# The end of each expert search moved from VectorE to GpSimd, with a store, the features, one search and six gathered steps placed elsewhere

## The reference

```python
q = (xb @ w_query).reshape(t, PEER_HEADS, 2, HALF_KEY)
s = jnp.einsum('thik,hink->thin', q, sub_keys)
v_half, i_half = lax.top_k(s, TOPK)                                # 16 best of 128 keys, in both halves
cand = v_half[:, :, 0, :, None] + v_half[:, :, 1, None, :]         # 16 x 16 pairs
cand_idx = i_half[:, :, 0, :, None] * N_KEYS + i_half[:, :, 1, None, :]
top_v, top_pos = lax.top_k(cand, TOPK)                             # 16 best pairs
idx = jnp.take_along_axis(cand_idx, top_pos, axis=-1)              # the expert's number
g = jax.nn.softmax(top_v, axis=-1)
act = jax.nn.gelu(jnp.einsum('thkd,td->thk', expert_u[idx], xb))
out = jnp.einsum('thk,thkd->td', g * act, expert_v[idx])
```

## Time and profile before

| | us |
|---|---|
| Three runs | 2607.22, 2611.05, 2610.92 (median 2610.92) |
| The profiled execution | 2620.58 |
| Its span | 2618.8 |
| First 64 u blocks on TensorE | 1458 to 1701 |
| Gates built | 1702 to 1837 |
| Rest of the u blocks and half of the v blocks | 1839 to 2283 |
| Last v blocks | 2283 to 2510 |
| End of the last gathered steps and results | 2619 |

### The profile page before, as it was taken

The page is one execution under the profiler, slowest core; times in us unless marked ns, Lnnn a source line. Parts: engine busy times, 40 slices in busy tenths (PEclk is TensorE's granted clock), DMA queues, the critical chain, the costliest instruction groups (busy, mean ns, idle before and its releaser), DMA issues.

```text
span 2618.8 us, 26507 instructions
## 1 busy us (share of the span) xinstructions
PE 2305.7 (88%) x8779; PEld 1454.0 (56%) x8779; DVE 1801.4 (69%) x3184; ACT 638.1 (24%) x1564; POOL 1169.0 (45%) x978
## 2 busy tenths in 40 slices
PE   6988888998899998899989988977999999999930
PEld 1545454454467443477568877856666666644410
DVE  2657676645501888777778997578766676757698
ACT  2334435331211113311321112199111100100010
POOL 0022222221000347666532334556548878676675
PEclk8999999999999998899999999999999999999975
DMA  8211101117575669999775679989999999999998
GB/s 303 73 33 57 40 24 40 49 60 272 195 269 182 229 254 383 361 339 415 287 265 185 225 257 334 348 305 362 352 394 411 412 386 418 347 419 378 419 395 296
DMA packets 235577, 705.28 MB, mean 269 GB/s; under 512 B 22910, under 2 KB 47614, under 8 KB 234052
## 3 DMA queue, kind: packets, MB, share of 16 engines
q0 software_dynamic: 117792, 428.92, 42.6%
q1 hardware_dynamic: 116948, 272.27, 27.9%
q10 hardware_dynamic: 720, 2.62, 0.2%
HBM read 690.23 MB, written 13.50 MB: 269 GB/s over the span
## 4 chain that ended last, share of the span: by engine, by line
PE 37%; DVE 19%; POOL 14%; DMA 11%; issue 11%; ACT 7%; SPq 1%; DVEq 0%; ACTq 0%; POOLq 0%; another core or an unknown queue 0%
PE bank L959 14%; POOL arena L1786 6%; POOL arena L1778 5%; DMA arena<-in_peer_v,arena 5%; PE bank L1181 4%; PE bank L808 4%; DMA arena<-in_peer_u,arena 3%; PE bank L853 2%; ACT arena L1674 2%; DVE arena L1964 2%; PE bank L1111 2%; DVE arena L2181 2%; POOL arena L1832 2%; DVE arena L2203 2%; DVE arena L2127 1%
## 5 line engine op out<-in xcount | busy, mean ns | idle before, releaser
L1778 POOL DMA_INDIRECT arena<-in_peer_u,arena x384 | 486.3, 1266 | 624.7 <-DVE arena L2181 346.0
L2203 DVE SCALAR_TENSOR_TENSOR arena<-arena 128x1024 f32<-128x1024 f32 x381 | 498.4, 1308 | 123.2 <-DMA arena<-in_peer_v,arena 113.6
L2181 DVE CUSTOM_DVE_ANT_0 arena<-arena 128x1024 f32<-128x1024 f32 x384 | 475.9, 1247 | 149.5 <-DMA arena<-in_peer_u,arena 147.5
L1786 POOL DMA_INDIRECT arena<-in_peer_v,arena x384 | 462.0, 1203 | 242.0 <-DVE arena L2203 132.4
L959 PE MATMUL bank<-arena 128*128 128x512 f32 (+1 forms) x1472 | 510.5, 509 | 21.8 <-issue 8.1
L1181 PE MATMUL bank<-arena 128*128 128x256 f32 x2048 | 457.2, 381 | 18.5 <-ACT arena L1633 17.8
L1219 PE MATMUL bank<-arena 128*128 128x512 f32 x1024 | 455.8, 598 | 7.2 <-DMA arena<-in_peer_v 4.0
L1181 PEld LDWEIGHTS bank<-arena 128*128 128x128 f32 x2048 | 391.7, 191 | 101.0 <-issue 49.4
L959 PEld LDWEIGHTS bank<-arena 128*128 128x128 f32 x1472 | 284.1, 194 | 244.1 <-issue 206.3
L1219 PEld LDWEIGHTS bank<-arena 128*128 128x128 f32 x1024 | 196.4, 192 | 228.1 <-issue 217.1
L1633 ACT ACTIVATE arena<-bank 128x256 f32<-128x256 f32 x128 | 49.0, 384 | 597.1 <-PE bank L1181 535.1
(11 more groups left out here) (259 smaller groups left out, 2469.6 us busy)
## 6 DMA issues: line engine op xcount, KB each, us to landing
arena<-in_peer_ut SPq DMA_DIRECT2D x128, 512.0 KB
arena<-in_peer_v SPq DMA_DIRECT2D x128, 512.0 KB
arena<-in_w_in SPq DMA_DIRECT2D x22, 2048.0 KB
arena<-in_w_ada_t POOLq DMA_DIRECT2D x32, 512.0 KB, 3.8
arena<-in_w_ssd_out SPq DMA_DIRECT2D x8, 2048.0 KB
arena<-in_w_query SPq DMA_DIRECT2D x8, 2048.0 KB
arena<-in_w_ada SPq DMA_DIRECT2D x4, 2048.0 KB, 16.3
arena<-in_w_fourier SPq DMA_DIRECT2D x4, 2048.0 KB
```

Source lines behind the costliest of these rows:

```text
L1778: nc.gpsimd.indirect_dma_start(rowbuf[slot], None, a["peer_u"], bass.IndirectOffsetOnAxis(ap=entries(IDX, k), axis=0)).then_inc(row_in[slo ...
L1786: nc.gpsimd.indirect_dma_start(rowbuf[slot], None, a["peer_v"], bass.IndirectOffsetOnAxis(ap=entries(IDX, k), axis=0)).then_inc(row_in[slo ...
L2181: V.tensor_tensor_reduce(out=rowbuf[slot], in0=rowbuf[slot], in1=h2c if item < PH else h2a[:, item // PH - 1, :], scale=1.0, scalar=0.0, o ...
L2203: STT(pv, rowbuf[slot], w, pv, ALU.mult, ALU.add).then_inc(s("vc_used"), 1)
```

## The change

1. **The search's end.** VectorE stops after the compare. It now casts the places to bf16 (L2237) and compares them with a table `places` of bf16 that is laid out in full, 16 wide (L2239). It raises `marked`. For the gathered tiles the numbers of the first half are multiplied by 128 while they are cast (`radix`). GpSimd does the rest in `picks_for`: multiply (L1819), adds of 8, 4 and 2 groups (L1821), and a last add into the whole numbers (L1823), or two adds and a cast into the rows' indices (L1826, L1828, L1829). Each waits for the one before it. VectorE waits for the end of one search before it overwrites the numbers in the next.
2. **Where GpSimd does it.** Ahead of each row's issue, all searches that VectorE passes before it frees that row's place are completed. The function `searches_before` works this out from a list of all searches.
3. **The store** of tile 0 goes from ScalarE's block 24 to GpSimd's apart step 28, with a semaphore of its own.
4. **The features** and the waits at ScalarE's block 31 go to block 35. `SOFTMAX_AT` goes from 8 to 10.
5. **44 steps** lie in the build instead of 38, and the search of heads 6 and 7 of tile 1 moves from step 94 to step 51, ahead of the build. What stands behind the build moves six steps with it.

The table `places` and several constants now share one buffer, `scan_consts`; the table is built just before the first search.

The core of the diff:

```diff
-SOFTMAX_AT = 8
+SOFTMAX_AT = 10
-IN_BUILD = 38
+IN_BUILD = 44
-APART_TOP_AT = {42 if n == 4 else START_BETWEEN if n == 6 else 16 * n - 14: (n, n + 1) for n in range(4, 2 * PH, 2)}
+APART_TOP_AT = {42 if n == 4 else 51 if n == 6 else 16 * n - 14: (n, n + 1) for n in range(4, 2 * PH, 2)}
...
-                if n == 24:
-                    store(0, 1)
-                if n == 31:
+                if n == 35:
                     act.wait_ge(s("topw_done"), 2 * PH)
...
+            def picks_for(kind, k):
+                while picks_done[0] < searches_before(kind, k):
+                    m, (items, _, _) = next(picked)
+                    n, (t, h) = len(items), divmod(items[0], PH)
...
+                    pool.wait_ge(s("marked"), m + 1)
+                    pch(TT(e4, e4, number.unsqueeze(3).broadcast_to([P, 2 * n, TOPK, TOPK]), ALU.mult))
+                    for m_left in (8, 4, 2):
+                        pch(TT(e4[:, :, 0:m_left], e4[:, :, 0:m_left], e4[:, :, m_left:2 * m_left], ALU.add))
+                    if t in WHOLE:
+                        TT(ij_all[:, :, TOPK * h:TOPK * h + TOPK], e4[:, :, 0, :], e4[:, :, 1, :],
+                           ALU.add).then_inc(s("topw_done"), n)
+                    else:
+                        pch(TT(picks[:, 0:2 * n * TOPK].rearrange("p (g k) -> p g k", g=2 * n), e4[:, :, 0, :], e4[:, :, 1, :],
+                               ALU.add))
+                        pch(TT(picks[:, 0:n * TOPK], picks[:, 0:n * TOPK], picks[:, n * TOPK:2 * n * TOPK], ALU.add))
+                        nc.gpsimd.tensor_copy(entries(IDX, items[0] * TOPK, n * TOPK),
+                                              picks[:, 0:n * TOPK]).then_inc(s("topk_done"), n)
             def u_row(k):
+                picks_for("u", k)
                 row_free("u", k)
...
             def v_row(k):
+                picks_for("v", k)
                 row_free("v", k)
...
+                        if j == 28:
+                            pool.wait_ge(s("out_ready"), 1)
+                            nc.gpsimd.dma_start(y_out[0:P, :], x1(0)).then_inc(s("out_0_done"), 16)
...
+                if searched["last"]:
+                    dve.wait_ge(s(searched["last"]), searched[searched["last"]])
...
-                ch(TT(e4, place.unsqueeze(2).broadcast_to([P, 2 * n, TOPK, TOPK]),
-                      flat(tijs).unsqueeze(3).broadcast_to([P, 2 * n, TOPK, TOPK]), ALU.is_equal))
-                ch(TT(e4, e4, flat(i16fs).unsqueeze(2).broadcast_to([P, 2 * n, TOPK, TOPK]), ALU.mult))
-                if t in WHOLE:
-                    V.tensor_reduce(ij_all[:, :, TOPK * h:TOPK * h + TOPK], e4, AX.X, ALU.add).then_inc(s("topw_done"), n)
-                else:
-                    ch(V.tensor_reduce(flat(picks), e4, AX.X, ALU.add))
-                    half = picks[:, 0:n * TOPK], picks[:, n * TOPK:2 * n * TOPK]
-                    STT(entries(IDX, items[0] * TOPK, n * TOPK), half[0], float(NKEY), half[1],
-                        ALU.mult, ALU.add).then_inc(s("topk_done"), n)
+                ch(CP(tij16s[:, 0:2 * n * TOPK], tijs[:, 0:2 * n * TOPK]))
+                TT(e4, places[:, 0:4:3 - n], flat(tij16s).unsqueeze(2).broadcast_to([P, 2 * n, TOPK, TOPK]),
+                   ALU.is_equal).then_inc(s("marked"), 1)
```

More of the change, by code:

```diff
@@ L222, with searches, searches_before @@
 START_LAST = START_BETWEEN + APART_BETWEEN
-APART_TOP_AT = {42 if n == 4 else START_BETWEEN if n == 6 else 16 * n - 14: (n, n + 1) for n in range(4, 2 * PH, 2)}
+APART_TOP_AT = {42 if n == 4 else 51 if n == 6 else 16 * n - 14: (n, n + 1) for n in range(4, 2 * PH, 2)}
+def searches():
+    at = [((0,), 0, 0), ((1,), 0, 0)] + [(pair, j + 1, 0) for j, pair in TOPS_AT.items()]
+    c, a = STEPS_DONE + 8, 0
+    for h in range(PH):
+        at.append(((3 * PH + h, 4 * PH + h), c, a))
+        c = min(CSTEPS, c + CTX_BESIDE[h])
+        if h in APART_TOP_BESIDE:
+            at.append((tuple(PH + n for n in APART_TOP_BESIDE[h]), c, a))
+        a += APART_BESIDE[h]
+    return at + [(tuple(PH + n for n in pair), CSTEPS, j + 1) for j, pair in sorted(APART_TOP_AT.items())]
+SEARCHES = searches()
+SEARCH_OF = {item: n for n, found in enumerate(SEARCHES) for item in found[0]}
+def searches_before(kind, k):
+    context, apart = 0, 0
+    before = ROW_BEFORE[ROW_NUMBER[kind, k]]
+    if before is not None:
+        kind_before, k_before = ROW_ORDER[before]
+        if k_before < PICKS:
+            context = k_before + 1 + (kind_before == "v") * LEAD
+        else:
+            apart = k_before - PICKS + 1 + (kind_before == "v") * APART_LEAD
+    passed = sum(c < context or a < apart for _, c, a in SEARCHES)
+    return max(passed, SEARCH_OF[k // TOPK] + 1)
 GATES_FIRST = (28, 36, 51)
@@ L503, in layer_kernel @@
         i16fs = small[:, 2].bitcast(BF16)
+        tij16s = small[:, 3].bitcast(BF16)
+        radix = small[:, 4, 0:2]
         dots = [small[:, 7, 0:TOPK], small[:, 11, 0:TOPK]]
@@ L736, in _ @@
                 load_block(n)
-            sp.wait_ge(s("out_done"), 16 * NT)
+            sp.wait_ge(s("out_0_done"), 16)
+            sp.wait_ge(s("out_done"), 16 * (NT - 1))
             sp.wait_ge(s("cst_out"), NG * 32 + 16)
@@ L1772, in row_free @@
                     pool.wait_ge(s("u_used" if kind_before == "u" else "vc_used"), k_before + 1)
+            pch = Chain(pool, s("pick"))
+            picked = iter(enumerate(SEARCHES))
+            picks_done = [0]
+            def picks_for(kind, k):
+                while picks_done[0] < searches_before(kind, k):
+                    m, (items, _, _) = next(picked)
+                    n, (t, h) = len(items), divmod(items[0], PH)
+                    e4 = cands[:, 0:256 * n].bitcast(BF16).rearrange("p (g m k) -> p g m k", g=2 * n, k=TOPK)
+                    number = i16fs[:, 0:2 * n * TOPK].rearrange("p (g m) -> p g m", g=2 * n)
+                    pool.wait_ge(s("marked"), m + 1)
[5 more added lines that the diff above has]
+                           ALU.add).then_inc(s("topw_done"), n)
+                    else:
+                        pch(TT(picks[:, 0:2 * n * TOPK].rearrange("p (g k) -> p g k", g=2 * n), e4[:, :, 0, :], e4[:, :, 1, :],
[3 more added lines that the diff above has]
+                                              picks[:, 0:n * TOPK]).then_inc(s("topk_done"), n)
+                    picks_done[0] = m + 1
             def u_row(k):
+                picks_for("u", k)
                 row_free("u", k)
@@ L2138, in scores_of @@
                 return src.rearrange("p (h n) -> p h n", h=2)
+            searched = {"topk_done": 0, "topw_done": 0, "last": None}
             def top(*items):
```

39 lines of the change are left out of this document (25 added, 14 removed).

## The result

The changed kernel is slower: ratio 1.023 to the kernel before, 95% interval 1.0203 to 1.0258, against a forecast of 1.009 with a range that ended at 2657 us. The median of the kernel before is 2610.99 us; the changed kernel's times are 2666 to 2678 us but for one execution of 3487 us, whose granted TensorE clock was 0.65 in all slices and of which the trace was recorded. The rows of after are therefore from a second run of the same kernel: 2668.98 us, ratio 1.0231 (1.0206 to 1.0256), span 2669.2 against 2618.8.

What follows compares the result with a forecast made beforehand. Build bound by ScalarE and almost as much by gathers, its start set by VectorE's chain of searches and context steps; +24.5 (build's end) - 1.1 (behind it) = +23.4: profiled 2644, median 2634 us (+0.9%), likeliest case 2616 to 2657, widened down to 2580.

Steps and rivals of the forecast that it cites:

- the transfer rate behind the build: Gathered steps after the build: sixteen take 69 us without a search, 76 with one, so 4.3 us a step.
- the four rivals: Shorter picks, 2577, 0.17; picks of 7 to 9 us, 2611, 0.14; build eats gain, 2596, 0.14; VectorE compare stays 1.22, +4.4.
- The meeting: GpSimd's picks beside VectorE's two-input operations: 8.5 us for a whole search, 11.7 for an apart one, VectorE 3.2 later.
- full exclusion: Upper bound for an apart pick: each of seven GpSimd operations waits out a 1.2 us VectorE operation, 13.8 us.
- The chain ahead of the build: Searches and context steps before the build: eighth whole search ends +17.8, TensorE reaches the build at about 1709.
- start of the first half: Early searches beside the latent projections: TensorE's wait there grows by +3 us (0 to 7).
- its gap ahead of the features: TensorE halts at 1592.3 and idles 24.1 us, against 17.8 in the kernel before, restarting at 1616.4.
- The build: Gates' build with 44 steps: takes 134 us, as long as before, and ends at 1861 against 1836.6, +24.5.
- The drain: VectorE's last gathered steps after TensorE stops: net +0.5 step done earlier, -1.1 us at 2.5 us a step.
- The rival of no meeting: Picks take 4.7 and 5.4 us undisturbed, both TensorE gaps go: together -34, 2577 us; chance 0.17.
- The store on GpSimd: Store of context's result at GpSimd's step 28: one more issue of about 1 us, hidden.
- six steps and the search at 51: In the rival of no meeting: 6 + 1.7 - 1.2 = 6.5 steps more done before the drain, -16.2 us.

Runs made afterwards that it cites:

- rest of the change: Kernel before plus store, features, softmax, 44 build steps and search at 51; no picks, VectorE's old search end: 2582.86 us, 0.9891.
- the new form on VectorE: Changed kernel with every search ended on VectorE (bf16 compare, multiply, adds by halves), 224 unused bytes putting the arena at 24320: 2583.19 us, 0.9904.
- the arena as before: Changed kernel, picks on GpSimd, with an unused buffer of 224 bytes a partition so the arena starts at 24320 again: 2639.35 us, 1.0114.
- the kernel with all ends on VectorE: Changed kernel with every search ended on VectorE in the change's form; with the arena moved (24096) 2626.61 us, 1.0048; at 24320 2583.19 us.

## Why the prediction was wrong

**The sum in one line.** Ratios of the runs give: rest of the change -1.0 to -1.1% (0.9891 with the old search, 0.9904 with the new form on VectorE), picks on GpSimd +2.1% (0.9904 to 1.0114), arena +1.2% (1.0114 to 1.0231; 1.1% in the kernel before, on one chip): -25 to -28, +55 and +30 us.

**What failed** is the transfer rate behind the build. The prediction took 4.3 us a step, and 402 GB/s for the build, from the rows of before, and had no term for the buffer `scan_consts`, which the text on the change named. I costed it at nothing without naming what would make that true. 16 steps took 71 and 72 us instead of 68 and 69 because of it: by the last v block the changed kernel had dotted 138 u rows of the second half where it does 145 with the arena as before, and its drain took 126.2 us instead of 102.1. That is 30 us by the end, of the 35 by which the forecast of 2634 us was below the 2669 measured. None of the four rivals was this.

**The meeting, right in mechanism and size.** Predicted 8.5 us for a whole search's pick beside four additions and 11.7 for an apart one beside eight operations; measured 8.4 and 11.5 where they meet as assumed. Alone: predicted 4.7 and 5.4, measured 4.8 and 5.4. VectorE's part, a cast of 0.25 and a compare of 0.69 us, measured 0.20 and 0.69, and its operations beside the apart pick lose 3.3 us together, 3.2 predicted. There was some luck in it: the earlier trace rows give 0.14 and 0.42 us an operation by the medians, 0.59 and 1.05 by the longest, and the 0.9 that I took was a choice near the upper end; measured 0.81 to 0.91.

I had set this against full exclusion at 13.8 us, and that bound was worked out wrongly. The rows above are those of two engines that take turns, one whole instruction at a time. GpSimd's multiply starts 1.05 us before VectorE's dot ends (1661.92 to 1663.14) and takes 0.91 more than alone; VectorE's addition, next, ends 1.08 us after the multiply, and alone lasts 1.28. So the two overlap by 0.2 us at the most. Each operation of GpSimd finds VectorE's already under way and waits out its rest, 0.81 to 0.91 us (0.86 on average for the three adds of the second row), and not a full 1.2. The Trainium skill, "SBUF — State Buffer", section "Who interferes with whom", states that of two such instructions the loser is blocked for the whole of the other; this trace agrees within those 0.2 us. A record's duration holds the wait too, so that the two records of the earlier trace rows lie over each other says nothing against it.

**The chain ahead of the build, right** where the arena is as before (third column of the table): start of the first half +3 predicted, +5.9 measured; TensorE ready for the build 1709 predicted, 1708.1 measured; its gap ahead of the features 24.1 predicted, 20.05 measured. The later start only shortens the gap: TensorE restarts at 1615.4, 1616.4 predicted. The pick behind step 42 ends at 1669.5 (1672.6 predicted) and that behind step 51 at 1723.1 (1724.1); in the changed kernel they end at 1673.6 and 1726.6. (Nine steps of 2.97 us from 1672.6 are 1699.3, where the prediction has 1698.7.) In the changed kernel the early part is 5.7 us later still. Whether that comes from the arena is not shown: the first u block is 10.2 us later with the arena moved in the kernel with all ends on VectorE, and 4.7 us earlier in the kernel before.

**The build** ended later by 28.9 us than before in that column, +24.5 predicted; at the last v block it is 27.4. **The drain** got 6.4 us shorter, 1.1 predicted: by the last v block three more steps are done than before, where I had half a step. The two misses cancel, which is luck: together the span is +21.0, +23.4 predicted. The ratio of that kernel, 1.0114, is +30 us, since the profiled execution of before was one of its slower ones; 2639.35 us stands beside a forecast of 2634. The forecast was of a change without its side effect.

**The rival of no meeting** (2577) was given 0.17. Its time is near that of the kernels whose ends stay on VectorE, 2583, but by another way; with the picks on GpSimd and their meetings taken away by a wait the time is 2649. The store on GpSimd was hidden, as said (an issue of 0.61 us); six steps and the search at 51 brought 0.8%, about 21 us, where I had written 16 for them in the rival.

**The best kernel of these** is the rest without the picks, 2582.86 us, 0.9891 (0.986 to 0.9923). The new form on VectorE adds nothing to that (0.9904).

## What to carry to other kernels

Before costing an edit of buffers at nothing, work out where every transfer's target starts after it, and compare the GB/s of a stretch in which the DMA share is 1.0 before and after: that row gives the arena's 30 us, half of the net loss, at a look. Work given to GpSimd is to be priced beside what VectorE does at that moment, not alone, and if GpSimd also issues the transfers, every microsecond of it is one in which no row is asked for (above, the next row's issue at 1673.72 follows the pick that began at 1662.09). A wait that keeps the two engines apart does not give the price back where both are on the chain.

## What the runs showed of the hardware

The start of the transfers' target within a partition set their rate. In the first 16 steps without a search behind the build, where the DMA share is 1.02 or 1.03 in every kernel, it is 412 to 419 GB/s in the six kernels with the arena at byte 24320, a multiple of 256, and 401 to 406 in the eleven with it 32, 64 or 128 bytes past a multiple of 256. The price was 0.9 to 1.4% of the time of the kernel before in the six pairs that differ in the start alone. The Trainium skill, "DMA: Bandwidth & Descriptors", section "How a descriptor splits into AXI transactions", states by the vendor's account that a descriptor is split into transactions of 256 bytes that must start on a 256-byte boundary. By that rule a row of 4096 bytes that starts 32 bytes past a boundary takes 17 transactions instead of 16, an estimate of 6% worked out from that page, or 129 beats of 32 bytes instead of 128, under 1%. The runs show 3 to 4%, between the two. They agree with the boundary in that 32, 64 and 128 bytes past it were all slow; but 24320 is the only multiple of 256 that was tried, so the boundary itself is not shown. Whether it counts for reads, writes or both wasn't tried, since only the side of the arena was moved.

GpSimd's operations on 32 elements take 0.21 to 0.25 us alone and 1.02 to 1.11 beside VectorE's dots and additions of two inputs, nearly the same for a cast as for an addition: each of them waits for most of one VectorE operation, and VectorE for GpSimd's longest (1.28 to 2.93 us beside the multiply). Beside VectorE's MAX8 and FIND_INDEX8, which read one input, the same multiply takes 1.91 us, as alone.
